# Half-block products for the first MLP matrix, and an MLP in two phases with its features kept in DRAM

## The chip, the cores and the metric

The kernel runs on one core of a Trainium2 chip (trn2). The metric is the device time of one execution in microseconds (us). The kernel before was timed three times.

## The reference, cut to what matters

The layer mixes tokens (gated linear attention, short convolution, pooling), adds the result to the stream `x`, and ends with a squared-ReLU MLP and an RMSNorm. Everything is float32, with 1024 tokens, 1024 model features and 4096 hidden features.

```python
mix = jnp.concatenate([y_gla, y_conv, y_pool], axis=-1) @ w_out
x = x + g1 * mix
h2 = modulate(x, norm2_w, sh2, sc2)                      # rmsnorm(x) * gain + shift
x = x + g2 * (jnp.square(jax.nn.relu(h2 @ w_mlp1)) @ w_mlp2)
return rmsnorm(x, final_norm_w)
```

The diff touches the start of the layer (first norm and first input products), the whole MLP, and the final norm.

## The kernel before, in words

Every float32 product is made from fp32r parts: an operand is split into a high part (ACT copies it with rounding) and a low part (DVE subtracts), and TensorE adds three matmuls, high times high, high times low and low times high. A feature tile is 128 features by 1024 tokens. A matmul writes 128 features by 512 tokens, half a tile.

There is no planner in this part: each engine runs its own list of instructions, written out by hand, in order, and waits on semaphores. All loads and stores are issued by SP on one queue. The order of each list is therefore the order of the work, and an instruction that waits holds back all that stand behind it on its engine.

**Start.** ACT squares the input, DVE adds the squares in two groups (`acc1`, `acc1b`), TensorE sums them over partitions with three groups of float32 matmuls (L832, L834). `modulation_rows(j)` and `modulation_turned(j)` make the modulation vectors (L811, L822). `scale1`, `low1` (DVE) and the ACT copies between them make the split input block by block, and `first_products(k)` (L975) multiplies block k for the gate tile and for the tile V0. POOL makes the low part of the first weight tile (L656).

**MLP.** After the output projection, `scale`, `high` and `low` make `h_hi` and `h_lo`, the split normed stream. Two hidden tiles are made directly (L1073 to L1079). Then eight chunks follow. A chunk makes four hidden feature tiles (two direct first products before `hid` is rewritten: `first_product`, L1081, 48 matmuls for each tile) and uses four tiles for the second product. The second product (`second_products`, L1091) goes by a seven-product scheme: two feature tiles (a pair, `kp`) by two token halves make a 2 by 2 block matrix, seven sums of its blocks (`t_made`, `t_high`, `t_low`) are multiplied by seven sums of weight blocks (`part_sums` on POOL, `w2_high` on ACT, `w2_low` on DVE). PSUM accumulates at most two of the seven before DVE has read it (`read`, L1994, which adds it to the residual `X` in SBUF). Each chunk has two halves `s` of 84 matmuls (7 products of 12) for the outputs. A product whose accumulator is used again waits for `read` (`ADDS_TO`, L70). So a chunk has 192 + 168 matmuls, and weights and hidden features never leave SBUF once loaded or made.

**End.** `square_out` (ACT), `sum_out` (DVE), two float32 sums on TensorE (L1134, L1136), then `scale_out` on DVE (5 and 6 of 8 blocks) and on POOL with ACT, and 16 stores issued by SP.

## Time and profile before

| what | us |
|---|---|
| median of three runs | 1164.92 (1164.52 to 1165.43) |
| profiled execution: its own time | 1164.41 |
| its span, first to last instruction | 1162.6 |
| PE (matmul) busy | 1109.3, 95% of the span, 5190 matmuls |
| DVE busy | 730.9, 63%, 915 instructions |
| ACT busy | 456.6, 39%, 701 |
| POOL busy | 248.2, 21%, 236 |
| HBM read and written | 83.74 MB and 4.19 MB, mean 76 GB/s |

The median of the runs is 0.5 us above the profiled execution, and 1.8 us of that execution lie outside the span. An engine's busy time is the union of its instructions' times. In the chain that ended last, lines of TensorE hold 86% of the span.

### The profile page before, as it was taken

How to read it: one execution, taken by the hardware profiler on the slowest of the kernel's cores; microseconds unless marked ns; L12 is line 12 of the kernel's file. 1: busy time of each engine (PE TensorE's matmuls, PEld its weight loads, DVE VectorE, ACT ScalarE, POOL GpSimd, SP SyncE). 2: the span in 40 equal slices, each digit the busy share in tenths (PEclk: the TensorE clock that was granted, in tenths of full speed). 3: DMA queues.
4: the chain of work that ended last, by engine and by line, in shares of the span. 5: the costliest groups of instructions: out<-in, count | busy, mean ns of one | idle time of the engine just before them, and what ended most of it. 6: DMA issues, size and time to landing. Idle time of an engine off the chain costs nothing.

```text
span 1162.6 us, 14199 instructions
## 1 busy us (share of the span) xinstructions
PE 1109.3 (95%) x5190; PEld 890.8 (77%) x5190; DVE 730.9 (63%) x915; ACT 456.6 (39%) x701; POOL 248.2 (21%) x236
## 2 busy tenths in 40 slices
PE   4899999999999999889999999999999999999995
PEld 1478888877887778578888888888888888888883
DVE  3777869646345875967548439358458366375486
ACT  5456524356525122463243243252332342432444
POOL 1100006386103262611101101202103011011033
PEclk9899999999999999899999999999999999999997
DMA  9423241101012751111211202102112101112003
GB/s 373 182 91 100 94 133 37 37 19 37 19 55 109 279 173 37 55 37 37 73 37 37 78 31 68 58 19 90 36 54 72 36 36 72 36 36 72 18 36 144
DMA packets 28437, 88.44 MB, mean 76 GB/s; under 512 B 2288, under 2 KB 3568, under 8 KB 27888
## 3 DMA queue, kind: packets, MB, share of 16 engines
q1 hardware_dynamic: 28400, 87.95, 21.4%
q8 instruction: 23, 0.38, 0.1%
q14 instruction: 14, 0.11, 0.0%
HBM read 83.74 MB, written 4.19 MB: 76 GB/s over the span
## 4 chain that ended last, share of the span: by engine, by line
PE 86%; DVE 6%; ACT 3%; DMA 2%; issue 1%; POOL 1%; SPq 0%; POOLq 0%; DVEq 0%; ACTq 0%
PE main L1087 28%; PE main L766 19%; PE main L1111 13%; PE sm L1111 8%; PE ob L1111 6%; PE main L981 2%; DVE xg L1911 1%; PE main L782 1%; PE ob L931 1%; DVE h_lo L1918 1%; DVE a_lo L1816 1%; PE sm L897 1%; PE sm L912 1%; PE ob L798 1%; PE ob L928 1%
## 5 line engine op out<-in xcount | busy, mean ns | idle before, releaser
L1111 PE MATMUL main<-tset,slot 128*128 128x512 f32 x672 | 157.9, 391 | 0.0
L1087 PE MATMUL main<-h_hi,w_hi 128*128 128x512 f32 x480 | 149.6, 393 | 1.3 <-DVE w_lo L1956 1.3
L1087 PE MATMUL main<-h_hi,w_lo 128*128 128x512 f32 x480 | 148.8, 391 | 0.0
L1087 PE MATMUL main<-h_lo,w_hi 128*128 128x512 f32 x480 | 148.4, 390 | 0.0
L1111 PEld LDWEIGHTS main<-tset,slot 128*128 128x128 f32 x672 | 125.6, 188 | 28.4 <-DVE X L2004 1.7
L722 POOL TENSOR_TENSOR part_sum<-raw 128x512 f32<-128x512 f32 x16 | 21.2, 1325 | 510.7 <-DMA raw<-wstream 510.7
L766 PE MATMUL main<-a_hi,w_hi 128*128 128x512 f32 x376 | 125.9, 416 | 2.7 <-DVE a_lo L1816 2.7
L766 PE MATMUL main<-a_lo,w_hi 128*128 128x512 f32 x376 | 116.6, 391 | 0.0
L766 PE MATMUL main<-a_hi,w_lo 128*128 128x512 f32 x376 | 116.2, 390 | 0.0
L1467 ACT ACTIVATE hid<-main 128x512 f32<-128x512 f32 (+1 forms) x48 | 35.3, 735 | 189.6 <-PE main L1087 189.6
L1087 PEld LDWEIGHTS main<-h_hi,w_hi 128*128 128x128 f32 x480 | 90.1, 188 | 21.3 <-DVE w_lo L1956 1.7
L1087 PEld LDWEIGHTS main<-h_lo,w_hi 128*128 128x128 f32 x480 | 90.1, 188 | 20.6
L1087 PEld LDWEIGHTS main<-h_hi,w_lo 128*128 128x128 f32 x480 | 90.2, 188 | 19.2
L1463 ACT ACTIVATE slot<-raw 128x512 fp32r<-128x512 f32 x80 | 47.6, 623 | 118.1 <-DMA raw<-wstream 63.2
L1111 PE MATMUL sm<-tset,slot 128*128 128x512 f32 x384 | 92.9, 391 | 0.0
L2004 DVE SCALAR_TENSOR_TENSOR X<-main,mods,X 128x512 f32<-128x512 f32 x112 | 79.9, 744 | 9.5 <-PE main L1111 9.1
L1111 PEld LDWEIGHTS sm<-tset,slot 128*128 128x128 f32 x384 | 72.1, 188 | 15.5
L766 PEld LDWEIGHTS main<-a_hi,w_hi 128*128 128x128 f32 x376 | 66.7, 188 | 21.1 <-issue 5.8
L766 PEld LDWEIGHTS main<-a_lo,w_hi 128*128 128x128 f32 x376 | 70.6, 188 | 15.6
L766 PEld LDWEIGHTS main<-a_hi,w_lo 128*128 128x128 f32 x376 | 70.6, 188 | 15.6
L1978 DVE TENSOR_TENSOR t_tmp<-hid,t_tmp 128x512 f32<-128x512 f32 x16 | 11.1, 692 | 103.2 <-ACT hid L1469 103.2
L1974 DVE TENSOR_TENSOR t_tmp<-hid 128x512 f32<-128x512 f32 x16 | 11.1, 692 | 100.9 <-ACT hid L1469 100.9
(285 smaller groups left out, 1887.3 us busy)
## 6 DMA issues: line engine op xcount, KB each, us to landing
raw<-wstream SPq DMA_DIRECT2D x60, 512.0 KB, 3.3
raw<-wstream SPq DMA_DIRECT2D x16, 1024.0 KB, 5.1
wmod<-wm SPq DMA_DIRECT2D x4, 2048.0 KB, 23.4
mbuf<-wm SPq DMA_DIRECT2D x16, 512.0 KB, 4.0
mbuf_late<-wm SPq DMA_DIRECT2D x16, 512.0 KB, 4.7
xs<-xt SPq DMA_DIRECT2D x8, 512.0 KB, 9.0
X<-xt SPq DMA_DIRECT2D x2, 2048.0 KB, 11.0
out<-X SPq DMA_DIRECT2D x16, 256.0 KB, 3.0
```

Of the source, the lines that this page charges most:

```text
L722: pool.tensor_tensor(held, a21, a22, ALU.add).then_inc(w2_sum, 1)
L766: ins = pe.matmul(main[:, bank, half * HALF:(half + 1) * HALF], w[:, slot, k, :], x[:, half * HALF:(half + 1) * HALF], start=begin, stop=end)
L782: ins = pe.matmul(main[:, bank, half * HALF:(half + 1) * HALF], w[:, slot, k, :], x[:, half * HALF:(half + 1) * HALF], start=begin, stop=end)
L798: ins = pe.matmul(ob[0:rows, (m % 2) * HALF:(m % 2) * HALF + NC], w(k), x[:, k, :], start=begin, stop=end)
L897: ins = pe.matmul(sm[:, b, q * DV:(q + 1) * DV], ktok[rows, h % 2, c // 2, :], vtok[rows, c // 2, h * DV:(h + 1) * DV], start=True, stop=True)
L912: ins = pe.matmul(sm[:, b, q * P:(q + 1) * P], ku[rows, h, t], qe[rows, h, t], start=True, stop=True)
L981: pe.matmul(main[rows, m, half * HALF:(half + 1) * HALF], w, x[:, k, half * HALF:(half + 1) * HALF], start=b, stop=e)
L1087: ins = pe.matmul(main[:, bank_pair, half * HALF:(half + 1) * HALF], w[:, slot, k, :], x[:, half * HALF:(half + 1) * HALF], start=begin, s ...
L1111: ins = pe.matmul(product_bank(s, acc, q), slot[:, w, q, kp, :], tset[j][:, kp, x, :], start=begins and kp == 0 and n == 0, stop=kp == 1 a ...
L1463: act.activation(slot[:, 0, :, :, :], operand(j), ACT.Copy).then_inc(w2_hi, 1)
L1467: act.activation(hid[:, t % 2, cols], main[:, 1 - t % 2, cols], ACT.Relu).then_inc(hid_relu, 1)
L2004: stt(out=X[:, m, cols], in0=product_bank(s, acc, q), scalar=mods[:, 3, m:m + 1], in1=X[:, m, cols], op0=ALU.mult, op1=ALU.add).then_inc(x ...
```

## The change

In phase 1 each pair of hidden feature tiles (15 pairs, `NMP` = 16 with the two tiles made directly) is made by seven half-block products of 12 matmuls, 84 where there were 96. The stream's blocks (two halves of the features, two token halves) get four split sums `h_sum[1, 2, 4, 6]`, made once. The weight sums are made for every pair on POOL (`part_sums1`), the seven splits on ACT (`w1_high`) and DVE (`w1_low`). Two accumulated products are first copied out (`copy_out`) or added (`add_out`) before an accumulator goes on. The seven sums of each pair's squared features are split into `stage` buffers and stored to DRAM (`hidden_kept`, seven stores of 512 KB for a pair). `X` is stored too (`x_kept`), as its place is needed. Phase 2 loads `X` and, for each chunk, seven sets of 1 MB from DRAM, and makes the second product as before. At the start, matmuls without use are added (`FILL`), the first products are put in another order, POOL's first low part moves to DVE. At the end the sums of one half are made before the last product.

```diff
+NMP = 16
+KP = KT // 2
+HID_ORDER = (0, 5, 2, 1, 4, 3, 6)
+HID_AT = {j: n for n, j in enumerate(HID_ORDER)}
+T_ORDER = (0, 3, 1, 5, 2, 4, 6)
+T_AT = {j: n for n, j in enumerate(T_ORDER)}
+SUMS = (2, 1, 4, 6)
...
+FILL = (16, 6)
...
+    def keep_hidden(pair, j):
+        sp.wait_ge(t_lo, pair * NPART + (T_AT[j] + 1))
+        sp.dma_start(hidden_kept[bass.ds(pair, 1), j].rearrange("a p c -> p (a c)"),
+                     stage[j][:, :, :].rearrange("p x n -> p (x n)").bitcast(F32)).then_inc(t_stored[j], 16)
+    def load_hidden(c, odd, j, nth=2):
+        if nth < 2:
+            sp.wait_ge(t_stored[j], c * 32 + 32)
+        if nth:
+            sp.wait_ge(t_loaded[j], c * 16)
+        sp.dma_start(tset[odd][j][:, :, :, :].rearrange("p k x n -> p k (x n)").bitcast(F32),
+                     hidden_kept[bass.ds(c * 2, 2), j].rearrange("k p c -> p k c")).then_inc(t_loaded[j], 16)
...
+    def period(i, at_b, at_a):
+        for j in T_ORDER[:2]:
+            keep_hidden(i - 1, j)
+        sp.wait_ge(w1_lo, i * NPART)
+        load_b(at_b)
+        for j in T_ORDER[2:]:
+            keep_hidden(i - 1, j)
+        if at_a is not None:
+            sp.wait_ge(w1_lo, i * NPART + 3)
+            sp.wait_ge(w1_sum, i * 4 + 4)
+            load_a(at_a)
+    for i in (1, 2):
+        period(i, stream1(i + 1) + 1, stream1(i + 2))
...
+    done = (NMP - 2) * NPART
+    for j in T_ORDER[:2]:
+        keep_hidden(NMP - 2, j)
+    sp.wait_ge(w1_lo, (NMP - 1) * NPART)
+    load_w2(T_MLP + 8, 0)
+    sp.wait_ge(x_stored[0], 16)
+    sp.wait_ge(hid_prod, done + HID_AT[0] + 1)
+    for m in range(4):
+        load_x(m)
+    for j in T_ORDER[2:]:
+        keep_hidden(NMP - 2, j)
+    for j, freed in enumerate((2, 2, 1, 1, 4, 3, 3)):
+        sp.wait_ge(hid_prod, done + HID_AT[freed] + 1)
+        load_hidden(0, 0, j, 0)
+    sp.wait_ge(x_stored[1], 16)
+    sp.wait_ge(x_stored[2], 16)
+    for m in range(4, KT):
+        load_x(m)
+    for j in T_ORDER[:2]:
+        keep_hidden(NMP - 1, j)
+    sp.wait_ge(w2_lo, NPART)
+    load_w2(T_MLP + 12, 0)
+    sp.wait_ge(hid_prod, done + NPART)
+    for j in range(3):
+        load_hidden(1, 1, j, 1)
+    for j in T_ORDER[2:]:
+        keep_hidden(NMP - 1, j)
+    sp.wait_ge(t_lo, NMP * NPART)
+    for j in range(NPART):
+        sp.wait_ge(t_stored[j], 16 * NMP)
+    for j in range(3, NPART):
+        load_hidden(1, 1, j, 1)
+    sp.wait_ge(w2_lo, 2 * NPART)
+    load_w2(T_MLP + 8, 1)
...
+    def chunk(c, odd, at, at_next):
         sp.wait_ge(w2_lo, c * (2 * NPART) + NPART)
         load_w2(at + 12, odd)
+        if at_next is not None:
+            sp.wait_ge(prod_done, c * (2 * NPROD))
+            for j in range(NPART):
+                load_hidden(c + 1, 1 - odd, j)
+            sp.wait_ge(w2_lo, c * (2 * NPART) + 2 * NPART)
+            load_w2(at_next + 8, 1 - odd)
...
+    def part_sums1(v, first=False):
+        pool.wait_ge(wa_loaded, v * 16 + 16)
+        pool.wait_ge(wb_loaded, v * 16 + 16)
+        if not first:
+            pool.wait_ge(w1_lo, v * NPART + (HID_AT[3] + 1 - NPART))
+        a11, a12, a21, a22 = quarter1(0, 0), quarter1(0, 1), quarter1(1, 0), quarter1(1, 1)
+        sums = held[:, :, :]
+        pool.tensor_tensor(sums, a21, a22, ALU.add).then_inc(w1_sum, 1)
+        pool.wait_ge(w1_sum, v * 4 + 1)
+        pool.tensor_tensor(a21, a11, a21, ALU.subtract).then_inc(w1_sum, 1)
+        pool.wait_ge(w1_sum, v * 4 + 2)
+        pool.wait_ge(w1_lo, v * NPART + (HID_AT[0] + 1))
+        pool.tensor_tensor(a11, sums, a11, ALU.subtract).then_inc(w1_sum, 1)
+        pool.wait_ge(w1_sum, v * 4 + 3)
+        pool.wait_ge(w1_lo, v * NPART + (HID_AT[1] + 1))
+        pool.tensor_tensor(sums, a12, a11, ALU.subtract).then_inc(w1_sum, 1)
...
+    def hidden_products(i, odd, nth=3):
+        for n, j in enumerate(HID_ORDER):
+            acc = PARTS[j][0]
+            pe.wait_ge(w1_lo, i * NPART + (n + 1 - NPART))
+            if nth == 1:
+                if j in SUMS:
+                    pe.wait_ge(sum_lo, SUMS.index(j) + 1)
+                elif j == 0:
+                    pe.wait_ge(mods_late, 2)
+                elif j == 5:
+                    pe.wait_ge(rs2_made, 2)
+            if j == 0 and nth == 3:
+                pe.wait_ge(hid_relu, i * 3 - 6)
+            if j == 5 and nth > 1:
+                pe.wait_ge(y_added, i * 3 - 5)
+            if j == 1 and nth > 1:
+                pe.wait_ge(y_added, i * 3 - 3)
+            if j in (2, 4, 3):
+                pe.wait_ge(y_copied, i * 3 + {2: -2, 4: -1, 3: 0}[j])
+            if j == 6:
+                pe.wait_ge(y_added, i * 3 - 1)
+            parts = h_set(j)
+            for kp in range(KP):
+                for m, (w, x) in enumerate(((0, 0), (0, 1), (1, 0))):
+                    ins = pe.matmul(hid_bank(acc, odd), slots1[j][:, w, kp, :], parts[x][:, kp, :],
+                                    start=PARTS[j][3] and kp == 0 and m == 0, stop=kp == KP - 1 and m == 2,
+                                    skip_group_check=True)
+            ins.then_inc(hid_prod, 1)
+    hidden_products(1, 1, 1)
+    hidden_products(2, 0, 2)
+    with pe.Fori(1, 7) as q:
+        hidden_products(q * 2 + 1, 1)
+        hidden_products(q * 2 + 2, 0)
+    hidden_products(NMP - 1, 1)
...
+    def last_sums(n, half):
         cols = slice(half * HALF, (half + 1) * HALF)
+        pe.wait_ge(acc3_made, 3 + 2 * n)
         pe.matmul(bank(2 + n), ones, acc2[:, cols], start=True, stop=False)
+        if n == 1:
+            pe.wait_ge(sq3_made, 11)
+            pe.matmul(bank(2 + n), ones, sqx[:, 5, cols], start=False, stop=False)
         pe.wait_ge(sq3_made, 4 + 4 * (n + 1))
         pe.matmul(bank(2 + n), ones, sqx[:, KT - 1, cols], start=False, stop=True).then_inc(sums3_done, 1)
+    chunk(0, 0, first=True)
+    with pe.Fori(0, 3) as q:
...
+    def w1_high(v, n, first=False):
+        j = HID_ORDER[n]
+        if j in (0, 5):
+            act.wait_ge(wa_loaded, v * 16 + 16)
+        elif j == 6:
+            act.wait_ge(wb_loaded, v * 16 + 16)
+        else:
+            act.wait_ge(w1_sum, v * 4 + {1: 1, 4: 2, 2: 3, 3: 4}[j])
+        if not first:
+            act.wait_ge(hid_prod, v * NPART + (n + 1 - NPART))
+        act.activation(slots1[j][:, 0, :, :], operand1(j), ACT.Copy).then_inc(w1_hi, 1)
...
+    act.wait_ge(late_turned, 2)
+    act.wait_ge(lo_made, LO_HID)
+    w1_high(0, 0, True)
+    w1_high(0, 1, True)
+    sum_high(2)
+    w1_high(0, 2, True)
+    sum_high(1)
+    w1_high(0, 3, True)
+    first_hidden(0)
+    sum_high(4)
+    w1_high(0, 4, True)
+    first_hidden(1)
+    sum_high(6)
+    w1_high(0, 5, True)
+    w1_high(0, 6, True)
...
+    def last_block(pair, odd):
+        act.wait_ge(hid_prod, pair * NPART)
+        relu_squared(odd, 1, 0, pair * 3, hid_bank(ACC_A, odd))
+    def t_high(pair, odd, j, nth=2):
         if j in (1, 2, 4, 6):
+            act.wait_ge(t_sum, pair * 4 + {1: 1, 2: 2, 4: 3, 6: 4}[j])
+        elif nth == 0:
+            act.wait_ge(hid0_sq, 2)
         else:
+            act.wait_ge(hid_sq, pair * 3 + {0: -2, 3: -1, 5: 0}[j])
+        if nth:
+            act.wait_ge(t_stored[j], pair * 16)
+        else:
+            act.wait_ge(sum_lo, len(SUMS))
+        act.activation(stage[j][:, 0, :], sources(odd)[j], ACT.Copy).then_inc(t_hi, 1)
+    def copy_out(i, odd, n, acc, at, row, half):
+        act.wait_ge(hid_prod, i * NPART + (at + 1 - NPART))
+        act.activation(hid_block(odd, row, half), hid_bank(acc, odd), ACT.Copy).then_inc(y_copied, 1)
+    def period(i, odd, nth=2, last=False):
+        prev, old = i - 1, 1 - odd
+        if nth > 1:
+            w1_high(prev, 6)
+            last_block(prev, old)
+        for j in T_ORDER[:2]:
+            t_high(prev, old, j, nth - 1)
+        if nth > 1:
+            act.wait_ge(t_lo, prev * NPART)
+        copy_out(i, odd, 0, ACC_A, 0, 0, 0)
         if not last:
+            w1_high(i, 0)
+        t_high(prev, old, 1, nth - 1)
+        t_high(prev, old, 5, nth - 1)
+        if not last:
+            w1_high(i, 1)
+        act.wait_ge(y_added, i * 3 - 2)
+        relu_squared(odd, 0, 0, i * 3 - 2)
+        t_high(prev, old, 2, nth - 1)
+        copy_out(i, odd, 1, ACC_A, 2, 0, 1)
+        if last:
+            w2_high(0, 0, True)
+        else:
+            w1_high(i, 2)
+        t_high(prev, old, 4, nth - 1)
+        t_high(prev, old, 6, nth - 1)
+        copy_out(i, odd, 2, ACC_C, 3, 1, 1)
+        if last:
+            w2_high(0, 1, True)
+        else:
+            w1_high(i, 3)
+            w1_high(i, 4)
+        act.wait_ge(y_added, i * 3 - 1)
+        relu_squared(odd, 1, 1, i * 3 - 1)
+        if last:
+            for j in range(2, 6):
+                w2_high(0, j, True)
+        else:
+            w1_high(i, 5)
...
+    tt(h_raw[1][:, :, :], xg[:, 1, 0:KP, :], xg[:, 0, 0:KP, :], ALU.subtract).then_inc(sum_made, 1)
+    w1_low(0, 0)
+    dve.wait_ge(sum_made, 1)
+    for k in range(KP):
+        stt(out=h_raw[2][:, k, :], in0=xg[:, 1, KP + k, :], scalar=mods[:, 1, KP + k:KP + k + 1],
+            in1=h_raw[1][:, k, :], op0=ALU.add, op1=ALU.subtract).then_inc(sum_made, 1)
+    w1_low(0, 1)
+    dve.wait_ge(sum_made, 5)
+    dve.wait_ge(x_stored[1], 16)
+    dve.wait_ge(x_stored[2], 16)
+    for k in range(KP):
+        stt(out=h_raw[6][:, k, :], in0=xg[:, 0, KP + k, :], scalar=mods[:, 1, KP + k:KP + k + 1],
+            in1=h_raw[2][:, k, :], op0=ALU.add, op1=ALU.subtract).then_inc(sum_made, 1)
+    dve.wait_ge(sum_made, 9)
+    sum_low(0)
+    w1_low(0, 2)
+    sum_low(1)
+    w1_low(0, 3)
+    dve.wait_ge(dif_made, 1)
+    for k in range(KP):
+        stt(out=h_raw[4][:, k, :], in0=xg[:, 1, KP + k, :], scalar=shift_dif[:, k:k + 1],
+            in1=xg[:, 1, k, :], op0=ALU.add, op1=ALU.subtract).then_inc(sum_made, 1)
+    dve.wait_ge(sum_made, 13)
+    sum_low(2)
+    w1_low(0, 4)
+    sum_low(3)
+    w1_low(0, 5)
+    w1_low(0, 6)
+    def t_made(pair, odd, n, nth=2):
...
+    def period(i, odd, nth=2, last=False):
+        prev, old = i - 1, 1 - odd
+        for n in (1, 2, 3):
+            t_made(prev, old, n, nth - 1)
+        for j in T_ORDER[:2]:
+            t_low(prev, old, j)
+        if nth > 1:
+            w1_low(prev, 6)
+        t_low(prev, old, 1)
+        if not last:
+            w1_low(i, 0)
+        t_made(prev, old, 4, nth - 1)
+        add_out(i, odd, 0, ACC_B, 1, 0, 0)
+        t_low(prev, old, 5)
+        if not last:
+            w1_low(i, 1)
+        t_low(prev, old, 2)
+        if last:
+            w2_low(0, 0)
+        else:
+            w1_low(i, 2)
+        t_low(prev, old, 4)
+        t_low(prev, old, 6)
+        if last:
+            w2_low(0, 1)
+        else:
+            w1_low(i, 3)
+        add_out(i, odd, 1, ACC_A, 4, 1, 1)
+        if not last:
+            w1_low(i, 4)
+        add_out(i, odd, 2, ACC_C, 5, 0, 1)
+        dve.wait_ge(y_added, i * 3)
+        y = hid_block(odd, 0, 1)
+        stt(out=y, in0=y, scalar=0.0, in1=y, op0=ALU.max, op1=ALU.mult).then_inc(y_squared, 1)
+        if last:
+            for j in range(2, 6):
+                w2_low(0, j)
+        else:
+            w1_low(i, 5)
...
+    w2_low(0, 6)
+    for n in (1, 2, 3):
+        t_made(NMP - 1, 1, n)
+    for j in T_ORDER[:2]:
+        t_low(NMP - 1, 1, j)
+    dve.wait_ge(x_back[0], 64)
+    read(0, 0, 0)
+    t_low(NMP - 1, 1, 1)
+    t_made(NMP - 1, 1, 4)
+    t_low(NMP - 1, 1, 5)
+    read(0, 0, 1)
+    t_low(NMP - 1, 1, 2)
+    w2_low(1, 0)
+    read(0, 0, 2)
+    t_low(NMP - 1, 1, 4)
+    w2_low(1, 1)
+    read(0, 0, 3)
+    t_low(NMP - 1, 1, 6)
+    w2_low(1, 2)
+    for j in range(4, NPART):
+        read(0, 0, j)
```

## Rows read from the trace of the kernel before

**Rows 1.** Chain that ended last, in the MLP: start us, us, what.
```profile
507.56 22.27 PE main L1087 x96
...
625.91 2.72 PE ob L1111 x12
...
650.47 43.96 PE main L1087 x192
```

**Rows 2.** Stretches: us, PE, PEld, DVE, ACT, POOL busy, clock, DMA share, GB/s.
```profile
560.00:1120.00 560.00, 560.00 (x2449) 459.09 (x2448) 325.55 (x457) 194.94 (x302) 76.29 (x54) 1.00 0.15 50
```

**Rows 3.** Timeline of ACT in the MLP: start us, us, line, op, shapes, count.
```profile
502.53 1.01 ACT L1467 ACTIVATE hid<-main 128x1024 f32<-128x1024 f32 x1
...
694.54 0.60 ACT L1467 ACTIVATE hid<-main 128x512 f32<-128x512 f32 x1 [6.64 <-PE main L1087]
695.18 0.63 ACT L1469 ACTIVATE hid<-hid 128x512 f32<-128x512 f32 x1
698.43 1.66 ACT L1479 ACTIVATE tset<-hid 128x512 fp32r<-128x512 f32 x3
...
725.02 1.06 ACT L1454 ACTIVATE w_hi<-raw 128x1024 fp32r<-128x1024 f32 x1 [4.69 <-DMA raw<-wstream]
```

**Rows 4.** Timeline of DVE in the chunk from 650.
```profile
695.93 0.69 DVE L1978 TENSOR_TENSOR t_tmp<-hid,t_tmp 128x512 f32<-128x512 f32 x1 [7.06 <-ACT hid L1469]
696.54 0.69 DVE L1980 TENSOR_TENSOR hid<-hid 128x512 f32<-128x512 f32 x1
698.95 1.40 DVE L2004 SCALAR_TENSOR_TENSOR X<-main,mods,X 128x512 f32<-128x512 f32 x2
```

**Rows 5.** Timeline of POOL in the same chunk.
```profile
706.29 1.30 POOL L722 TENSOR_TENSOR part_sum<-raw 128x512 f32<-128x512 f32 x1 [51.22 <-DMA raw<-wstream]
709.25 1.32 POOL L726 TENSOR_TENSOR raw<-part_sum,raw 128x512 f32<-128x512 f32 x1
```

**Rows 6.** Timeline of SP's DMA issues in the same chunk.
```profile
701.12 0.38 SPq L573 DMA_DIRECT2D raw<-wstream  x1
721.77 0.33 SPq L569 DMA_DIRECT2D raw<-wstream  x1
```

**Rows 7.** Stretches in which a load of 1 MB lands, and many loads (columns of rows 2).
```profile
704.00:705.00 1.00, 1.00 (x6) 0.81 (x5) 1.00 (x3) 0.00 (x0) 0.00 (x0) 1.00 1.05 410
25.00:30.00 5.00, 3.17 (x20) 0.91 (x19) 1.66 (x2) 4.38 (x6) 0.74 (x1) 1.00 1.02 433
```

**Rows 8.** DMA issues by target: op, count, KB each, median us to landing.
```profile
wg<-wg_in SPq DMA_DIRECT2D x1, 128.0 KB, 16.1
```

**Rows 9.** Timeline of DVE before the first chunk.
```profile
496.14 3.39 DVE L1918 SCALAR_TENSOR_TENSOR h_lo<-xg,mods,h_hi 128x512 fp32r<-128x512 f32 x5
506.28 1.23 DVE L1956 TENSOR_TENSOR w_lo<-raw,w_hi 128x1024 fp32r<-128x1024 f32 x1 [0.25 <-ACT w_hi L1454]
```

**Rows 10.** Stretches around idle times of PE (columns of rows 2).
```profile
396.00:398.00 2.00, 1.21 (x5) 0.67 (x4) 1.34 (x2) 0.41 (x1) 0.00 (x0) 1.00 1.04 416
472.00:475.00 3.00, 0.00 (x0) 0.00 (x0) 3.00 (x2) 0.72 (x1) 2.88 (x2) 1.00 0.00 0
475.00:478.00 3.00, 1.62 (x3) 0.83 (x3) 3.00 (x3) 0.00 (x0) 2.50 (x1) 0.50 0.00 0
```

**Rows 11.** Chain that ended last, the start.
```profile
15.86 3.75 PE main L832 x4
20.46 2.15 PE main L832 x4
28.34 5.05 DVE xs L1618 x2
57.24 0.52 PE main L981 x2
```

**Rows 12.** Timeline of the end.
```profile
1147.63 7.34 DVE L2086 SCALAR_TENSOR_TENSOR X<-ob,small,X 128x512 f32<-128x512 f32 x11 [0.93 <-ACT ob L1555]
1148.41 11.46 SPq L610 DMA_DIRECT2D out<-X  x16
```

More of the change, by code:

```diff
@@ L1538, in _ @@
             for m in range(4):
                 square_out(NPROD, m, slice(0, N))
-            for half, reads in ((1, (7, 8, 9, 10)), (0, (11, 12, 13, 14))):
-                for read, m in zip(reads, (4, 6, 5, 7)):
-                    square_out(NPROD + read, m, slice(half * HALF, (half + 1) * HALF))
             def scale_out(n, half):
@@ L2057, in _, with chunk @@
-            chunk(0, first=True)
+            def chunk(c, last=False):
+                for s in range(2):
+                    u = c * 2 + (s + 1)
+                    read(c, s, 0)
+                    for j in range(1, NPART):
+                        if last and s == 1 and j > 3:
+                            break
+                        read(c, s, j)
+                        if not (last and s == 1):
+                            w2_low(u, j - 1)
+                    if not (last and s == 1):
+                        w2_low(u, NPART - 1)
```

626 lines of the change are left out of this document (336 added, 290 removed).

## Prediction, made before the changed kernel was run

> **What bounds the kernel now.** I read the table of busy times first: TensorE is busy 95% of the span, and its lines hold 86% of the chain that ended last. Then the chain itself, stretch by stretch. From 560 to 1120 TensorE never idles, at full clock, while DVE is busy 58% of the stretch, ACT 35% and the DMA engines 15% [rows 2]. In the MLP the chain is nothing but matmuls: 192 in 43.96 us for four hidden tiles, 2.72 for each product of 12 [rows 1]. So a matmul taken out there saves 0.229 us, as long as nobody makes TensorE wait. The question is whether the lists of ACT, DVE, POOL and SP still keep ahead.
>
> **The matmuls removed.** A pair of hidden tiles cost 43.96 / 2 = 21.98 us and will cost 7 x 2.72 = 19.04. Fifteen pairs: 15 x 2.94 = **-44.1 us**. The second product keeps its matmuls.
>
> **Prices used below.** ACT starts 0.1 after its matmuls end (650.47 + 43.96 = 694.43, start 694.54); a block copy of 512 follows the one before it by 0.52 and ends 0.62 after its start, relu then square take 1.27 to the square's end [rows 3]. DVE starts 0.1 after ACT, 0.60 from block to block, 0.66 where it reads PSUM [rows 4]. POOL's first three sums take 706.29 to 710.57, 4.28, with DVE at work beside it; at its least 1.3 each, 3.9 [rows 5]; I take 4.0. SP issues a 512 KB load at 721.77 and ACT has it at 725.02: 3.25 [rows 3, 6]. At full share the DMA engines move 410 to 433 GB/s [rows 7]; I take 410: 2.56 us for 1 MB (1.05 million bytes), 1.28 for 512 KB, so 2.0 of the 3.25 is latency. That loads go in the order of issue: the 128 KB for `wg` landed 16.1 us after its issue, behind the 7 MB issued before it, which take 17.9 at 410 [rows 7, 8].
>
> The Trainium skill has two rules on this. DMA: Bandwidth & Descriptors (Queues, rings and completion order) says that SP's transfers share one ring on each DMA engine, whose descriptors are taken in ring order; by it, and the trace agrees (16.1 us for 128 KB), a small load waits for all that was issued before it, which is the rule that speaks most against this change. The same page (Where 436 GB/s comes from) lets the HBM side bind at about 358 GB/s; here the rows show 410 and more, so the measurement decides. By 358 each MB takes 2.93, and the 18 MB of the transition below would take 6 us longer.
>
> **The wait that comes in every pair.** Let 0 be the moment when TensorE ends a pair. ACT's list: `w1_high` of product 6, relu and square of the last block, `t_high` 0 (ends 2.4) and 3 (2.9). DVE's: `t_low` 0 from 2.5, `t_low` 3, `w1_low` of product 6, done at 4.4. Only then does SP issue `load_b` (4.6), behind two stores of 512 KB issued at 3.3 and 3.9. Their bytes move from 5.0 to 7.6, the load's to 8.9, landed at 9.2. POOL: three sums to 13.3. ACT's `w1_high(i, 2)` needs the third, and behind it stand `t_high` 4, `t_high` 6 and the third `copy_out`: it starts at 13.4 + 3 x 0.52 = 15.0, ends 15.6. TensorE's sixth product (j = 3) waits for that copy (`y_copied`) and could start at 5 x 2.72 = 13.6. So 2.1 us lost in each pair. With nothing ahead in the queue (landed 7.85, POOL 3.9) it is 0.7; with the measured 4.28 on POOL and a little more contention 2.6. For pairs 2 to 14: 13 x 2.1 = **+27 us** (9 to 34). Otherwise a pair fits: DVE has 19 x 0.60 + 3 x 0.66 = 13.4 and ACT 23 x 0.52 = 12.0 in 19.04.
>
> **Before the first pair.** `h_lo` is done at 499.5 [rows 9] and TensorE begins the next tile at 507.56 [rows 1]. DVE then makes the sums: one block of 2048 columns, 2.3 (1024 took 1.23, less overlap, twice [rows 9]), twelve of 512 with a scalar at 0.66, four `sum_low` at 2.3, and `w1_low` between. With no wait, `sum_low(2)` could begin at 516.9; it waits for ACT's `sum_high(4)`, of 2048 columns (1.06 for 1024 [rows 3]), to 519.0. Then ACT does `w1_high`, `first_hidden(1)` (relu and square of 1024, 2.1) and `sum_high(6)`, to 523.6, and DVE `sum_low(3)`, to 526.0. ACT's first `t_high` waits for all four `sum_lo`, and behind it stands `copy_out` 0, which ends at 527.8. But TensorE's third product of pair 1 waits for just that copy. It could start at 507.56 + 5.44 = 513.0. Lost: 14.8. In the same pair `load_b` is issued at 530.6 only, and the chain above ends at 541.6 where the sixth product could start at 536.0: 5.7 more. Together **+20.5 us** (17 to 24).
>
> **Between the phases.** S is TensorE's start on pair 15. From S + 3.3 SP issues, in this order: two stores of pair 14, `w2` (1 MB), `X` 0 to 3 (2 MB), five stores (2.5 MB), then the seven sets of chunk 0 (7 MB), `X` 4 to 7 (2 MB), two stores of pair 15 (1 MB), and then the second `w2` load (1 MB). That is 17.5 MB; bytes move from S + 5, at 2.56 a MB, so that the last lands at S + 50.1. The first set, behind 6.5 MB, lands at S + 24.5, and TensorE wants it at S + 19.0: 5.6 lost. DVE's list has `w2_low(1, 0)`, which needs that second load, ahead of `read(0, 0, 2)`. DVE stands at it from S + 27 to S + 50.9. The fifth product (j = 4) needs that read, could start at S + 35.5, and starts at S + 52.4: 16.9 lost. Behind it again: 3 sets (7.7 us), five stores (6.4), and after the last store has landed (S + 64.2) four sets (from 65.9 to 76.1) and the third `w2` load, landed at S + 79.0; `w2_low(2, 0)` holds the reads once more, and the product that could start at S + 71.5 starts at 81.3: 9.8 lost. Sum **+32 us** (25 to 40).
>
> **The chunks of phase 2.** 7 MB go behind the first `w2` load of a chunk, to 24.6 after its start; the other `w2` load then lands at 28.2, DVE's read is done at 29.6, TensorE wants it at 29.9. So 0 us, but 0.3 from a wait: +2 for each chunk if a set takes 10% longer. Six or seven such chunks: 0 to +14, I take 0.
>
> **What I cost at nothing.** The stores of `X`, 4 MB or 10 us of queue: SP issues them while TensorE is at the last output tiles and the two direct tiles, and nothing but the weights of pair 1 stands behind them, due 20 us later. If that cover is gone, `load_b` of pair 1 is late by at most the 2.6 of the last store, which DVE's sums still hide.
>
> **The clock.** After 3 us without a matmul the clock was granted at half, 0.50 of full, that is 1.2 GHz [rows 10]. What a start at the low clock costs, the first sums show: four matmuls in 3.75 instead of 2.15, about 2 us in all with the ones beside them [rows 11]. Five stops above are over 3 us: **+10 us** (4 to 12).
>
> **Start and end.** The added matmuls keep TensorE at work before the first sums, which saves nothing there (the next group of squares is ready at 20.2) and costs 6 x 0.6 less the 2.0 of slack, 1.6. POOL's low part no longer runs beside DVE's first scaling: 5.05 for two [rows 11] become 1.5 each, and only the first stands before ACT. The modulation rows come earlier and find the clock up. Going through the lists in the same way, the point that TensorE reached at 57.24 [rows 11] comes at 52: **-5 us** (0 to -8). At the end DVE scales 11 blocks in 7.34 after the last sum and SP issues 16 stores in 11.46 [rows 12]; five of the blocks and their stores now come before or during it: **-4 us** (-2 to -6).
>
> **Sum**, against the profiled execution's own 1164.4: -44.1 + 27 + 20.5 + 32 + 0 + 10 - 5 - 4 = +36.4, so 1200.8; the median of the runs lies 0.5 above that execution: **1201 us**. Its own range, with not all terms at one end: 1180 to 1222.
>
> **The rivals.**
> 1. *The queue does not hold the loads* (other side, faster). If a load issued behind others lands nearly as soon as alone, 7.85 in a pair and 5 us after issue between the phases, the pair's wait is 0.8 (+10), the transition 2, the first pair 19, the clock 4: 1164.9 - 44.1 + 10 + 19 + 2 + 4 - 9 = **1147**. The point from which it decides: the waits of pairs and transition together under 26 us instead of 59. For it: a pair moves 4.5 MB, 11.5 us of its 19, so the DMA engines are free for a good part of it. Against it: the 16.1 us of `wg` [rows 8], and that 1 MB takes 2.56 whatever the order [rows 7].
> 2. *Only the transitions cost.* The wait in the pairs is gone or near it (+5), since stores and load overlap or POOL is quicker without DVE: 1164.9 - 44.1 + 5 + 20 + 32 + 8 - 9 = **1177**.
> 3. *The clock falls in every pair.* If 2.1 us of idle are enough for a half clock, each of 13 pairs loses 2 more: 1201 + 26 = **1227**. For it: the clock was down at 475 after 3 us [rows 10]. Against: two gaps of together 0.8 us at 396 to 398 left it at full [rows 10]; nothing between is shown.
>
> **How the numbers follow.** Forecast 0.50, rival 1 0.20, rival 2 0.16, rival 3 0.14. A measurement of this kernel can tell about 0.2%, 2.3 us, from no change. Faster is rival 1 and a little of the others: 0.22; within 0.2%: 0.03; slower: 0.75. The range 1150 to 1230 takes in rival 2, most of 3 and part of 1.
>
> **What would show it.** In the trace after: 84 matmuls for a pair in about 21.1 us with one gap of 2 before the sixth product, ended by ACT's third copy; ACT's `w1_high` of j = 2 waiting for POOL; a gap of 15 us before the third product of pair 1; two stops in the first chunk of phase 2 with DVE waiting for ACT and ACT for a DMA; after that chunks of 38 us without gaps. The forecast is wrong if SP's `load_b` comes much before 4.6 after a pair's end, or if DMA shares in the transition are under 0.8 while the load is out.

## The result and the profile after

The changed kernel takes **1249.56 us** (median of 4 runs, 1249.38 to 1253.12), the kernel before beside it 1164.72 (1164.46 to 1165.43): ratio 1.0736, 95% interval 1.0719 to 1.0753. The prediction had 1201 with a range of 1150 to 1230: the direction is right, the size is not, 85 us instead of 36.

First the stretches of the changed kernel, cut where the order of the work changes: the start, the first pair up to its sixth product, pairs 2 to 14 (sixth product to sixth product), one pair of these, the way to phase 2, the first chunks, the others. Columns as in [rows 2].

```profile
0.00:500.50 500.50, 479.11 (x2441) 373.31 (x2442) 338.10 (x364) 216.29 (x330) 144.40 (x166) 0.99 0.32 114
500.50:539.60 39.10, 17.14 (x62) 13.21 (x61) 28.41 (x34) 22.21 (x29) 5.46 (x4) 0.74 0.27 94
539.60:852.60 313.00, 275.31 (x1093) 219.79 (x1093) 190.72 (x287) 166.88 (x300) 66.80 (x52) 0.92 0.54 196
709.64:733.60 23.96, 21.12 (x84) 16.85 (x85) 14.66 (x23) 12.83 (x24) 5.15 (x4) 0.93 0.54 197
852.60:886.20 33.60, 25.59 (x108) 20.03 (x109) 25.08 (x35) 20.25 (x37) 7.26 (x5) 0.98 0.80 304
886.20:950.00 63.80, 42.13 (x147) 33.06 (x148) 29.53 (x41) 8.09 (x13) 10.93 (x8) 0.77 0.80 317
950.00:1228.50 278.50, 276.75 (x1188) 222.78 (x1187) 218.69 (x297) 64.11 (x102) 79.22 (x55) 1.00 0.54 207
```

Where the kernel before had TensorE busy from end to end at clock 1.00 [rows 2], pairs 2 to 14 now show 275 of 313 us at a clock of 0.92. A pair takes 24.1 us where 7 products alone take 19.04. What TensorE waited for most from 500 to 950, in us, times, longest:

```profile
PE sm L1313 <- ACT hid L1773: 42.9, 15, 4.4
PE ob L1313 <- ACT hid L1773: 17.6, 1, 17.6
PE main L1351 <- DVE XR L2414: 14.3, 1, 14.3
PE sm L1351 <- DVE XR L2414: 7.4, 1, 7.4
PE main L1351 <- DMA tset<-hidden_kept: 6.0, 1, 6.0
```

All five are waits that the prediction named: L1773 is the third copy of each pair (42.9 us, of which 37.7 in pairs 2 to 14) and the first copy of pair 1 (17.6), the others are the three stops between the phases. One pair as the chain of waits has it (start, length, what): the weight load is out for 5.5 us, then come POOL's three sums, ACT's list down to the copy, and only then the sixth product:

```profile
720.56 0.70 DVE slot L2272
721.47 5.49 DMA raw<-wstream
...
727.18 1.29 POOL held L875
...
730.00 1.28 POOL raw L880
...
732.98 0.49 ACT hid L1773
733.47 0.14 issue
733.60 4.53 PE sm L1313 x12
738.13 2.81 PE ob L1313 x12
```

The sixth product takes 4.53 us where twelve matmuls took 2.72 before [rows 1]. Two stretches of 1 us show why: the clock is at full when it starts and at half (1.2 GHz) behind it.

```profile
734.00:735.00 1.00, 1.00 (x6) 0.76 (x5) 0.99 (x2) 0.50 (x1) 0.22 (x1) 0.85 0.79 311
735.00:736.00 1.00, 1.00 (x4) 0.81 (x3) 1.00 (x2) 0.64 (x2) 1.00 (x1) 0.50 1.00 406
```

This half clock lasts 3.4 us and comes with the stop before the sixth product in 12 of the 13 pairs from 2 to 14, once for 6.8 us. In pair 14, whose stop was 2.5 us, it does not come.

| term, against the kernel before | predicted | measured |
|---|---|---|
| matmuls removed | -44.1 | -44.1 (as reckoned) |
| pairs 2 to 14: 13 x 5.03 (24.07 - 19.04) | +27 | +65.4 |
| pair 1 to its sixth product | +20.5, clock 4 | +25.3 |
| between the phases, and the chunks | +32, clock 6 | +49.1 |
| start | -5 | -6.9 |
| end (from the last but one product) | -4 | -1.4 |
| time of the kernel before's MLP beyond 2.72 us a product (21.98 for a pair) | 0 | -2.4 |
| sum | +36.4 | +85.0 |

The last column is read from starts of products: pair 1 begins at 500.7 (507.6 before), the last but one product of the MLP at 1225.3 (1138.8 before). The first row is the prediction's own reckoning at 2.72 us a product; what the products of the changed kernel took beyond that is in the rows below it. Of the 49 us between the two sums, 38 lie in pairs 2 to 14 and 11 in the row between the phases (49.1 for 32 + 6).

### The profile page after: what moved, and what is told of

It is laid out like the page before. It is cut to its first block, busy times and chain, and to the rows that moved or that the text cites. A ratio compares the mean times of both kernels' runs of the same rounds, so it can differ in the third digit from the quotient of the medians.

```text
span 1247.7 us, 15400 instructions
## 1 busy us (share of the span) xinstructions
PE 1123.0 (90%) x5056; PEld 885.9 (71%) x5056; DVE 841.3 (67%) x1068; ACT 507.2 (41%) x823; POOL 320.3 (26%) x295
## 4 chain that ended last, share of the span: by engine, by line
PE 28%; DMA 13%; POOL 5%; ACT 4%; issue 4%; DVE 3%; SPq 0%; ACTq 0%; POOLq 0%; DVEq 0%
PE main L1351 12%; DMA raw<-wstream 11%; PE sm L1351 5%; PE sm L1313 5%; PE ob L1313 3%; PE ob L1351 3%; ACT stage L1768 1%; POOL raw L877 1%; POOL held L875 1%; POOL raw L880 1%; DVE stage L2347 1%; DMA tset<-hidden_kept 1%; DVE slot L2272 1%; ACT hid L1747 1%; DVE slot L2277 1%
## 5 line engine op out<-in xcount | busy, mean ns | idle before, releaser
L1351 PE MATMUL main<-tset,slot 128*128 128x512 f32 x672 | 165.3, 404 | 20.2 <-DVE XR L2414 14.3
L1313 PE MATMUL ob<-h_sum,slot 128*128 128x512 f32 x540 | 136.2, 402 | 18.8 <-ACT hid L1773 17.6
L1716 ACT ACTIVATE slot<-raw 128x512 fp32r<-128x512 f32 x80 | 50.2, 630 | 233.0 <-DMA raw<-wstream 139.2
L1313 PEld LDWEIGHTS ob<-h_sum,slot 128*128 128x128 f32 x540 | 106.0, 197 | 44.1 <-DVE slot L2272 18.0
L1313 PE MATMUL sm<-h_hi,slot 128*128 128x512 f32 x240 | 95.2, 462 | 42.9 <-ACT hid L1773 42.9
L2272 DVE TENSOR_TENSOR slot<-raw,slot 128x512 fp32r<-128x512 f32 x75 | 61.4, 819 | 78.3 <-ACT slot L1704 78.3
L2277 DVE TENSOR_TENSOR slot<-raw,slot 128x512 fp32r<-128x512 f32 x80 | 62.8, 803 | 59.8 <-ACT slot L1716 59.8
L1313 PEld LDWEIGHTS sm<-h_hi,slot 128*128 128x128 f32 x240 | 53.2, 222 | 60.9 <-DVE slot L2272 47.5
L2414 DVE SCALAR_TENSOR_TENSOR XR<-main,mods,XR 128x512 f32<-128x512 f32 x112 | 80.8, 743 | 22.0 <-PE main L1351 21.2
L1704 ACT ACTIVATE slot<-raw 128x512 fp32r<-128x512 f32 x75 | 46.9, 627 | 113.1 <-POOL raw L880 72.4
L937 PEld LDWEIGHTS main<-a_hi,w_lo 128*128 128x128 f32 x376 | 70.6, 188 | 15.7
L875 POOL TENSOR_TENSOR held<-raw 128x512 f32<-128x512 f32 x15 | 19.8, 1321 | 219.0 <-DMA raw<-wstream 219.0
L1351 PE MATMUL ob<-tset,slot 128*128 128x512 f32 x288 | 71.0, 395 | 0.0
```

The lines of the kernel that those rows point to most:

```text
L875: pool.tensor_tensor(sums, a21, a22, ALU.add).then_inc(w1_sum, 1)
L937: ins = pe.matmul(main[:, bank, half * HALF:(half + 1) * HALF], w[:, slot, k, :], x[:, half * HALF:(half + 1) * HALF], start=begin, stop=end)
L1313: ins = pe.matmul(hid_bank(acc, odd), slots1[j][:, w, kp, :], parts[x][:, kp, :], start=PARTS[j][3] and kp == 0 and m == 0, stop=kp == KP ...
L1351: ins = pe.matmul(product_bank(s, acc, q), slots2[j][:, w, q, kp, :], tset[odd][j][:, kp, x, :], start=begins and kp == 0 and n == 0, stop ...
L1704: act.activation(slots1[j][:, 0, :, :], operand1(j), ACT.Copy).then_inc(w1_hi, 1)
L1716: act.activation(slots2[j][:, 0, :, :, :], operand(j), ACT.Copy).then_inc(w2_hi, 1)
```

## The experiments

All are the changed kernel with one edit or a few; the times are medians, each beside runs of the kernel before on the same chip (1164.3 to 1164.5). The changed kernel is 1249.6.

**1. The load ahead of the stores.**

```diff
     def period(i, at_b, at_a):
-        for j in T_ORDER[:2]:
-            keep_hidden(i - 1, j)
         sp.wait_ge(w1_lo, i * NPART)
         load_b(at_b)
-        for j in T_ORDER[2:]:
+        for j in T_ORDER:
             keep_hidden(i - 1, j)
```

> The changed kernel, with SP's weight load of a pair issued ahead of both stores that stood before it; nothing else is moved. Theory (the load waits in the queue behind the two stores, and the stop that follows lets the clock fall): the load still goes out 4.5 us after the pair's last matmul, but lands 3.3 later instead of 5.5; the stop before the sixth product shrinks from 2.9 to about 0.7 us and the half clock behind it (3.4 us long, 1.7 us lost) is gone. A pair takes 24.07 - 2.2 - 1.7 = 20.2 us, 13 pairs save 50, pair 1 saves 2 to 4: 1197 us. Rival 1 (a load of 512 KB takes 5.5 us beside this traffic wherever it stands): pairs stay at 24, 1249. Rival 2 (the clock falls in every pair because of the load on the chip, not because of the stop): the stop goes and the half clock stays, 22 us a pair, 1221.

Measured: 1214.3 us, ratio 1.0433 (1.0413 to 1.0454), 35 less. In one pair (the only one from 2 to 14 that kept its half clock) SP's issues, POOL's first sum and the end of TensorE's stop:

```profile
700.83 0.35 SPq L648 DMA_DIRECT2D raw<-wstream  x1
...
701.44 11.49 SPq L657 DMA_DIRECT2D hidden_kept<-stage  x7
...
705.19 1.82 POOL L873 TENSOR_TENSOR held<-raw 128x512 f32<-128x512 f32 x1 [12.11 <-DMA raw<-wstream]
...
712.17 0.66 PE L1311 MATMUL sm<-h_hi,slot 128*128 128x512 f32 x1 [2.00 <-ACT hid L1771]
```

The load lands 4.1 us after its issue (3.8 to 5.1 in pairs 2 to 14), between the 5.5 that it took in the changed kernel and the 3.25 of a lone one: what stands ahead counts for 1.4. The other 0.8 comes with the stores right behind it; that they are its cause is argued, not shown. The stop is 1.4 to 2.4 us, the half clock is gone from all but one of pairs 2 to 14, a pair takes 21.4. The mechanism holds; that the whole 2.2 would be won does not.

**2. Two buffers for the seventh product's weights**, with edit 1.

Cut to the main lines:

```diff
+    slot6 = [slots1[6], at("slot1_6b", [P, 2, KP, P], F32R, ZA + 56 * KIB)]
     def period(i, odd, nth=2, last=False):     # ACT; DVE likewise
         if nth > 1:
-            w1_high(prev, 6)
             last_block(prev, old)
...
         else:
             w1_high(i, 5)
+            w1_high(i, 6, odd=odd)
```

> The changed kernel with two buffers in turn for the split weights of the seventh product, so that ACT and DVE make them at the end of the pair's list, before TensorE is done with the pair before; SP issues the weight load as soon as they are made, ahead of the two stores. Theory (the whole chain hangs on the one weight block that can't be split before TensorE ends the pair): the load goes out about 0.5 us before the pair's end instead of 4.5 after it, all of its 5 us are won, no stop before the sixth product, clock full: a pair takes 7 products, 19.1 to 19.4 us, 13 pairs save 61 to 64, pair 1 saves 2 to 4: 1184 us. Rival (the next link is right behind, ACT's third copy or the traffic of 4.5 MB in 19 us): a stop of 1 to 2 us stays, 20.2 to 21 us a pair, 1197 to 1207.

Measured: 1185.3 us, 1.0189 (1.0171 to 1.0207), 64 less. From pair 2 to the end of pair 14 TensorE never stops:

```profile
560.00:800.00 240.00, 240.00 (x1040) 194.52 (x1039) 205.53 (x274) 160.34 (x285) 70.87 (x48) 1.00 0.62 238
```

A pair takes 19.4 us with all of its 4.5 MB of traffic. So the stop came from one weight block that could not be split before TensorE had ended the pair, and neither the traffic nor DVE's list (now 86% busy, 16.6 us a pair where the prediction had 13.4) takes its place. It also gives the true price of the products: without any stop a pair takes 0.4 us more than the 19.04 of the prediction.

**3. The stop filled with matmuls of no use.**

```diff
     def hidden_products(i, odd, nth=3):
...
+            if j == 3 and nth > 1:
+                for k in range(12):
+                    pe.matmul(bank(0), slots1[3][:, k % 2, k % KP, :], h_set(3)[0][:, k % KP, :], start=True,
+                              stop=True, skip_group_check=True)
             if j in (2, 4, 3):
                 pe.wait_ge(y_copied, i * 3 + {2: -2, 4: -1, 3: 0}[j])
```

> The changed kernel with 12 matmuls of no use before the wait of the sixth product, in pairs 2 to 15 (they write a free PSUM bank). They take 2.7 us, which is the length of the stop. Theory (1.7 us of each pair are the clock, which falls because TensorE stands still): the stop is filled, the clock stays full in pairs 2 to 14, a pair takes 24.07 - 1.7 = 22.4 us, 13 pairs save 22, pair 15 loses 2, as its stop was only 0.8: 1230 us. Rival (the clock falls because of the power drawn or has nothing to do with the stop): the half clock stays and the added matmuls cost nothing or up to 2.7 us a pair, 1249 to 1285.

Measured: 1231.3 us, 1.0579 (1.0558 to 1.06), 18 less, with more matmuls than the changed kernel. The pairs:

```profile
600.00:840.00 240.00, 239.30 (x1031) 192.81 (x1030) 156.69 (x235) 136.10 (x244) 56.92 (x44) 1.00 0.58 210
```

TensorE stands for 0.7 of 240 us and the clock is at full; a pair takes 22.6 us. The added work costs nothing there, as it lies where TensorE stood; what is won is the price of the clock alone, 1.4 us for each of 13 pairs, net of what the filler costs where the stop was shorter.

**4. ACT's third copy ahead of the late weight block.**

```diff
+    copy_out(i, odd, 2, ACC_C, 3, 1, 1)
     if last:
         w2_high(0, 0, True)
     else:
         w1_high(i, 2)
     t_high(prev, old, 4, nth - 1)
     t_high(prev, old, 6, nth - 1)
-    copy_out(i, odd, 2, ACC_C, 3, 1, 1)
```

> The changed kernel with ACT's third copy of a pair ahead of the split of weight block j = 2, which waits for POOL; nothing else is moved, the weight load is as late as before. Theory (the stop belongs to the order of ACT's list as much as to the late load): the sixth product starts without a wait, 2.9 us earlier and at full clock, and TensorE waits before the seventh instead, for DVE's second addition, which stands behind the same late weight block and ends about 1 us earlier than now: the seventh product starts some 3 us earlier than in the changed kernel, after a stop of 1.5 us that leaves the clock up. A pair takes about 21 us instead of 24.07, 13 pairs save 40: 1210 us. Rival (the stop before the seventh product is as long as the one before the sixth was, and the clock falls as before): 24 us, 1245 to 1250.

Measured: 1219.7 us, 1.0474 (1.0452 to 1.0495), 30 less. What TensorE waited for from 550 to 870:

```profile
PE ob L1313 <- DVE hid L2354: 23.5, 14, 2.4
```

The wait for ACT is gone and DVE's second addition (L2354) has taken its place, shorter (1.1 to 2.4 us). The clock still fell behind five of these stops (1.85 to 2.40 us), 5 x 1.7 = 8.5 of the 10 us that are missing against the expectation; a pair takes 22.1 on average, 21.6 from pair 4 on. Two repairs at different ends of one chain, the load (1) and the copy that stood behind its product (4), win about the same.

**5. The first copy of pair 1 alone moved forward.**

```diff
     first_hidden(0)
+    copy_out(1, 1, 0, ACC_A, 0, 0, 0)
     sum_high(4)
```

> The changed kernel with ACT's first copy of pair 1 made right after the first hidden tile, ahead of the sum of j = 4, instead of behind all of the preparation; nothing else is moved. TensorE's stop of 17.6 us before its third product ends with this copy. Theory (the first pair is bound by a second chain: DVE's list ends with the split of the last weight block at 523.3, then the weight load, POOL's sums and the third copy, which let the sixth product start at 539.6): the third product starts at about 508.5, 15 us earlier, the time saved turns into a stop before the sixth product, and the whole gains 0 to 3 us: 1246 to 1250. Rival (the 17.6 us are lost in themselves): 15 us less, 1234.

The copy is left out of its old place. Measured: 1251.9 us (1250.9 to 1254.6), nothing won. TensorE's waits from 490 to 560:

```profile
PE ob L1313 <- ACT hid L1731: 19.1, 2, 17.2
```

The third product starts after a stop of 1.9 us, and the stop of 17 stands two products later, at the second copy. The longest wait of the whole profile was worth nothing by itself. (I had expected it before the sixth product, so the next link was nearer than I thought.)

**6. to 8. SP's list between the phases**, in three steps: (6) the second `w2` load behind the fourth set of chunk 0, the third ahead of the last four sets of chunk 1; (7) also two sets ahead of the `X` blocks, and the third `w2` load ahead of the waits for the stores; (8) also all sets of chunk 1 behind it. Edit 8 as a whole:

```diff
+    for j in T_ORDER[2:5]:
+        keep_hidden(NMP - 2, j)
     sp.wait_ge(x_stored[0], 16)
-    sp.wait_ge(hid_prod, done + HID_AT[0] + 1)
+    sp.wait_ge(hid_prod, done + HID_AT[2] + 1)
+    load_hidden(0, 0, 0, 0)
+    load_hidden(0, 0, 1, 0)
     for m in range(4):
         load_x(m)
-    for j in T_ORDER[2:]:
+    for j in T_ORDER[5:]:
         keep_hidden(NMP - 2, j)
-    for j, freed in enumerate((2, 2, 1, 1, 4, 3, 3)):
+    for j, freed in ((2, 1), (3, 1), (4, 4), (5, 3), (6, 3)):
         sp.wait_ge(hid_prod, done + HID_AT[freed] + 1)
         load_hidden(0, 0, j, 0)
+        if j == 3:
+            sp.wait_ge(w2_lo, NPART)
+            load_w2(T_MLP + 12, 0)
...
-    sp.wait_ge(w2_lo, NPART)
-    load_w2(T_MLP + 12, 0)
     sp.wait_ge(hid_prod, done + NPART)
-    for j in range(3):
-        load_hidden(1, 1, j, 1)
     for j in T_ORDER[2:]:
         keep_hidden(NMP - 1, j)
+    sp.wait_ge(w2_lo, 2 * NPART)
+    load_w2(T_MLP + 8, 1)
     sp.wait_ge(t_lo, NMP * NPART)
     for j in range(NPART):
         sp.wait_ge(t_stored[j], 16 * NMP)
-    for j in range(3, NPART):
+    for j in range(NPART):
         load_hidden(1, 1, j, 1)
-    sp.wait_ge(w2_lo, 2 * NPART)
-    load_w2(T_MLP + 8, 1)
```

> The changed kernel with two of SP's loads between the phases moved: the second load of second-product weights goes behind the fourth of the seven sets of chunk 0 (it was behind all seven, four blocks of X and two stores), the third goes ahead of the last four sets of chunk 1. Theory (DVE's list holds the reads behind these weights, and the loads land in the order of issue): the second load lands about 15 us earlier, the stop of 14.3 us in the first chunk shrinks to 2 or 3 and the one of 7.4 to 0 or 1, and two half clocks go, worth 4 to 5: together about -22, 1227 us. Rival (the bytes of the transition are the bound, in whatever order): TensorE waits as long for the sets instead, 1245 to 1250.

> The changed kernel with SP's list between the phases in the order in which the data are wanted: two sets of chunk 0 ahead of the X blocks, the second load of second-product weights after the fourth set, the third one right behind the stores of pair 15, ahead of the waits for their landing. In the run before, with only the first two moved, the third load was held by those waits to 927.7, 15 us after DVE had freed its place. Theory: no stop of 6 us before chunk 0, none of 14, the one of 7 down to 0 to 3, and three half clocks (8 us lost) gone: 30 to 35 us less than the changed kernel, 1217 us. Rival (DMA engines are at full share from 878 to 925, so the bytes bind): what one stop loses another gets, 1235 to 1245.

> transition2 with one more move: the first three of the seven sets of chunk 1 go behind the third load of second-product weights, with the other four. In transition2 that load was issued at 916.1 and landed at 933, behind three sets and five stores, and TensorE stood 12 us. Theory (the queue is served in the order of issue and is full; what may wait has to be issued last): 3 MB less ahead of it are 7.7 us at 410 GB/s, the load lands at about 923 to 925, the stop of 12 shrinks to 1 to 4 us and its half clock (2.9 lost) may go: 8 to 14 us less than transition2, 1225 to 1231 us. Rival (chunk 1 then waits for its sets instead): 1235 to 1240.

Measured: 1241.0, 1239.0 and 1233.6 us (1.0666, 1.0628 and 1.0591, each +-0.0018), so 9, 11 and 16 less than the changed kernel where 22, 33 and 18 to 24 were expected. (7) came out as its rival had it (1235 to 1245), (6) and (8) between theory and rival. In (6) the stop of 14 us goes and the one of 7.4 grows to 13.9, since its load was held by the waits for the stores. In (7) that load goes out at 916 and still lands at 933; SP's issue (its timeline), and then two stretches of (7):

```profile
916.05 1.20 SPq L652 DMA_DIRECT2D raw<-wstream  x1
```

```profile
878.00:906.00 28.00, 21.85 (x81) 16.64 (x81) 21.45 (x30) 10.82 (x20) 7.70 (x6) 0.88 1.03 406
906.00:926.00 20.00, 17.71 (x76) 13.92 (x74) 11.73 (x19) 2.42 (x4) 1.29 (x1) 1.00 1.03 413
```

For 48 us the DMA engines are full: here the bytes bind, and reordering only helps where something can be put off past the queue's end. That is (8), whose two longest waits from 850 to 960 are

```profile
PE sm L1354 <- DVE XR L2417: 4.6, 1, 4.6
PE main L1354 <- DMA tset<-hidden_kept: 4.4, 1, 4.4
```

against 14.3, 7.4 and 6.0 in the changed kernel. In (7) 1 MB issued into a full queue took 17 us to land. The Trainium skill, DMA: Bandwidth & Descriptors (Queues, rings and completion order), has each DMA engine take its descriptors in ring order; these runs agree.

**9. Without the matmuls added at the start.**

```diff
-FILL = (16, 6)
+FILL = (0, 0)
```

> The changed kernel without the 22 added matmuls at the start. The start gained 7.1 us where the prediction had 5, with a price of 1.6 for these matmuls. The prediction's account: without them the start is 0 to 1.6 us shorter, 1248 to 1249.5. Rival (they keep the clock up where TensorE works between waits, in the kernel before it was at half from 31.3 to 34.7 and 38.1 to 44.9, in the changed one only from 38.4 to 41.8): without them the start is 1 to 4 us longer, 1251 to 1253.

Measured: 1252.3 us (1251.4 to 1253.4), 2.7 more by the medians, but the runs overlap. At the start the clock is at half for 6.8 us instead of 3.4, but among kernels that do have these matmuls it was at half there for anything from 0 (experiment 1) to 6.8 us (6 and the last one below). The long stop of pair 1 ended at 527.9 us, in other kernels with an unchanged start anywhere from 524.0 to 527.7. So the theory's 0 to 1.6 us less did not show, and whether these matmuls keep the clock up stays open.

**10. to 12. Together.** Two buffers (2), edit 7 and a first pair with two copies early and the last three weight blocks split ahead of the sums; then two buffers with all three copies and DVE's second addition early in pair 1; then this with edit 8. ACT's part of the first pair in the last two:

```diff
     first_hidden(0)
+    copy_out(1, 1, 0, ACC_A, 0, 0, 0)
+    act.wait_ge(sum_made, 13)
+    w1_high(0, 4, True)
+    w1_high(0, 5, True)
+    w1_high(0, 6, True)
     sum_high(4)
-    w1_high(0, 4, True)
+    copy_out(1, 1, 1, ACC_A, 2, 0, 1)
+    copy_out(1, 1, 2, ACC_C, 3, 1, 1)
     first_hidden(1)
     sum_high(6)
-    w1_high(0, 5, True)
-    w1_high(0, 6, True)
```

> The changed kernel with the two buffers for the seventh product's weights, the load ahead of the stores, the order between the phases of transition2, and a first pair in which ACT copies the first and second sum out early and the last three weight blocks are split ahead of the sums of the stream, so that the load goes out at about 516. Theory: the gains add up, 1249.5 - 64 (as measured for the two buffers) - 33 - 14 = 1138 us, 26 us faster than the kernel before. Rival (without stops in the pairs, the 4.5 MB of each in 19 us and the 17 MB of the transition meet the DMA engines' limit, or the next link of the first pair takes over): 1150 to 1165.

> The changed kernel with the two buffers for the seventh product's weights, the load ahead of the stores, and a first pair in which all three copies of pair 1 and DVE's second addition go ahead of the splitting of the hidden tiles made directly, and the last three weight blocks are split ahead of the sums of the stream. In the kernel with only two of the copies early, the sixth product of pair 1 stood 9.2 us for the third copy, behind POOL. Theory: TensorE waits for the sum of the stream for j = 4 (5 us) and for DVE's second addition before the seventh product (2 to 4 us), and the pair ends about 10 us earlier than with the two buffers alone: 1185.3 - 10 = 1175 us. Rival (the stop only moves on to the next link again, as with the first copy alone): 1182 to 1187.

> first_pair2 and transition3 in one kernel. Theory: the gains add up: 1185.3 (two buffers) - 10 (first pair) - 20 (transition, of which 10.5 were measured with transition2) = 1155 us, about 9 us or 0.8% faster than the kernel before. Rival (where the pairs have no stops, the stores of pair 15 and the loads of the transition come together more densely, and a part of the gain is given back): 1162 to 1168, no faster than before.

Measured: 1173.5 (1.0071, 1.0054 to 1.0088), 1182.0 (1.0156, 1.0141 to 1.0172) and, in 11 runs, **1162.4 us (0.9984, 0.9974 to 0.9993)**. The last is 0.16% faster than the kernel before, just beyond its interval and under the 0.2% of the prediction: the repaired scheme draws level. The first missed its theory (1138) and its rival (1150 to 1165) alike; the other two came out as their rivals had it. The first pair gave 3 us instead of 10, as its stops move from link to link (in the last kernel 5.3 for the sum of j = 4, 4.1 for DVE's addition), and what remains is that and the transition:

```profile
PE sm L1354 <- DVE XR L2428: 6.0, 3, 4.0
PE ob L1316 <- DVE hid L2366: 5.3, 2, 4.1
PE ob L1316 <- DVE h_sum L2295: 5.3, 1, 5.3
PE main L1354 <- DMA tset<-hidden_kept: 4.6, 1, 4.6
```

## Why the prediction was wrong, step by step

- **The wait in every pair: right in its place, short in its size.** `load_b` goes out 4.55 us after the pair's end (4.6 predicted). It lands at 10.0 instead of 9.2, POOL's sums end at 14.4 (13.3), the product starts at 16.7 (15.7); with its five products a little slower, TensorE stood 2.8 us in this pair and 2.9 on average, not 2.1. What was mis-sized here is "the load's to 8.9": while the last store and the load were out the engines moved 250 and 221 GB/s at a full share, not 410.
- **The clock: this is the step that failed.** "Five stops above are over 3 us" gave no clock to the 13 stops of the pairs. 12 of them had a half clock, 11 for 3.4 us and one for 6.8. That is 44 us at half speed, of which TensorE worked for 43: 21 us lost. Experiment 3 shows the cause, as filling the stop brings the clock back. It stood there as rival 3 with 0.14, and only as an addition of 26 to the forecast. The pairs then are 27 + 10 for the longer stop (13 x 0.8) + 21 for the clock + 6 for matmuls that take longer than 2.72 us a product at full clock, 65.
- **A hint that was in the trace before.** The prediction weighed one stop of 3 us and two short gaps, and said that nothing between is shown. But twice in the kernel before the clock fell with no such stop: at 31.3, shortly behind a stop of 1.8 us and 8 matmuls of 2 columns, and at 458.0, shortly behind 3.5 us of matmuls of one column, without any stop at all:

```profile
29.72 1.05 PE L822 MATMUL sm<-fold,mrow 96*128 96x2 f32 x8 [1.83 <-ACT mrow L1164]
453.81 3.63 PE L1049 MATMUL ob<-small,macc_late 128*128 128x1 f32 x32
458.00:461.00 3.00, 3.00 (x9) 2.31 (x8) 0.00 (x0) 0.00 (x0) 0.00 (x0) 0.50 0.00 0
```

These rows speak for rival 3 and would have raised its chance. Nor did any of the signs that were to show the forecast wrong look at the clock: both concerned the queue, and neither came.
- **The range.** It went to 1230, which is rival 3 with every other term at its middle. The forecast's own range reached 1222 without the clock in the pairs; with it (26 more) it would have reached 1248. The two had not been joined, though a longer stop and a falling clock have the same cause.
- **Before the first pair: the waits right, the sum in part by luck.** 25.3 with its clock for 24.5. The stop was 17.6 where 14.8 were predicted. But the sixth product started 38.9 us after the start of pair 1, where the account of the waits had 34.0 (541.6 - 507.56), and the 4 us for the clock do not explain it: the half clock there slowed products 3 to 5, which were followed by a stop of 4.4 that took it up. What was longer is the chain: the load went out 26.2 us into the pair instead of 23.0 and took 6.1 us to land. And it is not 14.8 + 5.7 that one could win back: experiment 5 shows that the first wait alone is worth nothing.
- **Between the phases: right.** 6.0, 14.3 and 7.4 us for 5.6, 16.9 and 9.8, and 8 us lost at half clock for 6. What comes on top is 13 us: 2 in two short stops of pair 15, 2 to 3 around waits that hang on the `w2` loads of the chunks (the longest 1.1), put at 0 though the text saw them 0.3 us off, and some 8 in matmuls that come every 0.2345 us instead of 0.2267 in about two thirds of the chunks.
- **Start and end: near, the start by luck.** -6.9 for -5 is read at pair 1 (0 to 4 us less in other executions, by experiment 9). Just behind the first products, 76.7 us into the kernel before, only 3.3 were won; the rest came later, among it 1.3 from a wait before pair 1 that is gone. The end gave -1.4 for -4: SP issues its stores 4 us earlier against the last product, but the sums put ahead of this product hold it up by 1.3, and the 16 stores take 12.0 us instead of 11.5.
- **Rivals 1 and 2 fell.** The queue holds the loads (experiments 1, 7, 8), and the waits of pairs 2 to 14 and of the transition together are 37.7 + 27.7 = 65 us, where rival 1 needed under 26.
- **The matmuls removed: right in number, the saving put a little too high.** 2.72 us is the second product's twelve; the same rows have 2.75 for the first product's (43.96 / 16), and experiment 2 shows 19.4 for a pair instead of 19.04. So the change takes out some 38 us, not 44.1. The table has the difference in the rows below its first one.

## What to carry to other kernels

A short stop that comes back in every turn of a loop is not worth its length alone: once a stop is near those that have cost the clock, join it with the clock's price in the forecast and in its range. In a chain of lists written by hand look for the one buffer whose reuse starts the chain late; a second buffer there, with the load ahead of the stores, gave 64 us, nearly twice as much as either repair that moved one step (35 and 30). And a wait's length says nothing of what its removal gives until the next link is known.
